# Two experts with fixed places, their token lists made tile by tile, in a mixture-of-experts decoder step

## The reference

```python
def _post_norm_block(x, mix, ...):
    h = _layernorm(DN_ALPHA * x + mix, ln1_g, ln1_b)
    return _layernorm(DN_ALPHA * h + _moe(h, ...), ln2_g, ln2_b)
# _moe: group = argmax of 4 group logits; the 2 best of its 8 experts;
#   weight = p_group * softmax over the two; for each of the 32 experts, its tokens:
#   (silu(x @ w_gate[e]) * (x @ w_up[e])) @ w_down[e] * weight, summed into y[token]
```

## Time and profile before

| | |
|---|---|
| median of 3 runs | 1728.58 us (1725.63 to 1732.63) |
| profiled execution, span | 1724.0 us |
| TensorE / VectorE / ScalarE busy | 1657.2 / 657.7 / 348.0 us |
| HBM read, written | 307.90 MB, 35.51 MB |
| DMA queue of SyncE (q1) | 276.22 MB |
| DMA queue of POOL (q0) | 55.78 MB |

### The profile page before, as it was taken

The page is one execution under the profiler, slowest core; times in us unless marked ns, Lnnn a source line. Parts: engine busy times, 40 slices in busy tenths (PEclk is TensorE's granted clock), DMA queues, the critical chain, the costliest instruction groups (busy, mean ns, idle before and its releaser), DMA issues.

```text
span 1724.0 us, 22514 instructions
## 1 busy us (share of the span) xinstructions
PE 1657.2 (96%) x9293; PEld 1015.9 (59%) x9294; DVE 657.7 (38%) x1382; ACT 348.0 (20%) x679; POOL 163.5 (9%) x169
## 2 busy tenths in 40 slices
PE   8999999999999999999999999999999999999990
PEld 5556777777777666666688555554444444444440
DVE  1446454545542323232577654621121212121225
ACT  1113232223231222212212011111111111111115
POOL 1000000000003321121000000011111111111110
PEclk9999999999999999999899999999999999999995
DMA  7200121211017554342362522578999999999975
GB/s 228 61 21 20 50 62 50 59 53 50 23 64 209 190 170 142 123 158 88 128 218 75 210 104 79 202 302 327 374 394 375 393 397 386 386 390 391 390 289 202
DMA packets 104410, 337.67 MB, mean 196 GB/s; under 512 B 24378, under 2 KB 68482, under 8 KB 87924
## 3 DMA queue, kind: packets, MB, share of 16 engines
q1 hardware_dynamic: 89572, 276.22, 42.4%
q0 software_dynamic: 13568, 55.78, 10.7%
q10 hardware_dynamic: 1168, 4.23, 0.6%
HBM read 307.90 MB, written 35.51 MB: 199 GB/s over the span
## 4 chain that ended last, share of the span: by engine, by line
PE 91%; DMA 5%; DVE 2%; issue 1%; ACT 1%; SPq 0%; POOL 0%; DVEq 0%; POOLq 0%; ACTq 0%
PE psum L1058 12%; PE psum L1172 10%; PE psum L1478 8%; PE psum L1483 7%; PE psum L1360 6%; PE psum L1375 5%; PE psum L1510 4%; PE psum L1504 4%; PE psum L1099 4%; PE psum L962 3%; PE psum L1211 3%; PE psum L1072 2%; DMA arena<-in_w_up 2%; PE psum L1117 2%; PE psum L1491 2%; PE psum L1106 2%
## 5 line engine op out<-in xcount | busy, mean ns | idle before, releaser
L1058 PE MATMUL psum<-arena 128*128 128x258 f32 x896 | 215.3, 384 | 0.0
L1172 PE MATMUL psum<-arena 128*128 128x344 f32 x576 | 182.3, 458 | 0.0
L1058 PEld LDWEIGHTS psum<-arena 128*128 128x128 f32 x896 | 162.8, 190 | 27.9 <-issue 7.0
L1483 PE MATMUL psum<-arena 128*64 128x512 f32 x320 | 141.6, 595 | 0.7 <-ACT arena L1809 0.7
L1484 PE MATMUL psum<-arena 128*64 128x512 f32 x320 | 141.6, 595 | 0.0
L1478 PE MATMUL psum<-arena 128*128 128x512 f32 x320 | 139.8, 595 | 0.2 <-DVE arena L2559 0.2
L1172 PEld LDWEIGHTS psum<-arena 128*128 128x128 f32 x576 | 103.2, 190 | 53.0 <-issue 11.2
L1478 PEld LDWEIGHTS psum<-arena 128*128 128x128 f32 x320 | 60.0, 190 | 72.6 <-issue 72.1
L1360 PE MATMUL psum<-arena 128*128 128x258 f32 x448 | 99.7, 387 | 0.9 <-ACT arena L1766 0.9
L1375 PE MATMUL psum<-arena 128*128 128x512 f32 x224 | 99.2, 595 | 0.0
L1360 PEld LDWEIGHTS psum<-arena 128*128 128x128 f32 x448 | 86.5, 193 | 14.2 <-issue 1.3
(11 more groups left out here) (391 smaller groups left out, 2147.8 us busy)
## 6 DMA issues: line engine op xcount, KB each, us to landing
arena<-in_w_gate SPq DMA_DIRECT2D x32, 2048.0 KB, 20.6
arena<-in_w_up SPq DMA_DIRECT2D x32, 2048.0 KB, 26.3
arena<-in_w_down SPq DMA_DIRECT2D x32, 2048.0 KB, 32.6
arena<-in_w_in SPq DMA_DIRECT2D x33, 512.0 KB, 4.9
gates<-arena SPq DMA_DIRECT2D x16, 516.0 KB, 6.0
arena<-gates SPq DMA_DIRECT2D x16, 516.0 KB, 6.4
arena<-in_x_prompt SPq DMA_DIRECT2D x16, 512.0 KB, 4.6
arena<-in_w_o SPq DMA_DIRECT2D x1, 4096.0 KB, 17.0
```

The costliest lines, as they stand in the source:

```text
L1058: ins = mm(psum[:, BANK[name[0]], 0:QT], held, moved, start=(k == 0 and name in ("X1", "V6", "Y5")), stop=(k == 3), skip_group_check=True)
L1172: ins = mm(psum[:, FB + t, 0:SP3], wring[:, u, k, :], xT[:, k, t * SP3:(t + 1) * SP3], start=(k == 0), stop=(k == KD - 1))
L1483: g = mm(psum[0:64, 2, :], xgT[:, xpar, k, 0:64], wg[:, k, :], start=(k == 0), stop=(k == KD - 1))
```

## The change

1. The two fixed experts come first, then `h h f m ...`; `SOON`, the number of experts with a list of their own, falls from 3 to 2. Their three early matrices and the next three go to other ring places.
2. Their lists are made tile by tile. As their numbers are known, no rank is needed: `first_positions(n)` on TensorE gives each token of tile n its place in the two lists, `first_rows(n)` on VectorE makes a one-hot of it, `first_table(n)` adds the tile to the lists. L1468 and its one-hots are gone.
3. The slot tables of all experts run behind gate and up of the first expert and the turn of the second's rows; VectorE's arithmetic for them lies around the first expert's operations (`swiglu` is cut into `swiglu_gate` and `swiglu_up`, and the copies behind the tables are `slot_lists`).
4. The second expert's matrices are loaded as four parts of 32 partitions each (`load_parts`), without a wait for the row DMAs, the third of them after the lists (`tb_done`). The place under `oh_row` is now that of the third expert's down matrix.
5. `sums` gets `h` unscaled; the weights are divided by ALPHA and the last norm's eps by its square, which leaves the norm's result as it was.
6. Fewer `keep_busy`.

```diff
-SOON = 3
+SOON = 2
-        ring_at = [Z0, Z0 + MAT, Z3 - 64 - 2 * MAT] + [Z3 + i * MAT for i in range(6)] + [Z3 - 64 - MAT]
+        ring_at = [Z3 + i * MAT for i in range(6)] + [Z0, Z0 + MAT, Z3 - 64 - 2 * MAT, Z3 - 64 - MAT]
-        RANK = [next(kinds["h"])] + list(range(FIXED)) + [next(kinds[c]) for c in "hfmhfmhfmhmhfmhfmhfmhfmhmfmqq"]
+        RANK = list(range(FIXED)) + [next(kinds[c]) for c in "hhfmhfmhfmhmhfmhfmhfmhfmhmfmqq"]
@@ SyncE @@
+            def load_parts(j, e):
+                for c in range(4):
+                    part = slice(32 * c, 32 * c + 32)
+                    sp.dma_start(ring(j)[part], matrix(j % 3, e)[part]).then_inc(we_ld[j % RING], 16)
             sp.wait_ge(lg_done, NT)
             sp.wait_ge(h_dve, NT)
+            for m in range(2):
+                load_parts(3 + m, 1)
+            sp.wait_ge(tb_done, 1)
+            load_parts(5, 1)
+            sp.wait_ge(h_out, 16 * NT)
             for q in range(2):
                 sp.wait_ge(ah_out[q], 16 * ((NT - q + 1) // 2))
-            for m in range(3):
-                load_matrix(6 + m, 1)
-            sp.wait_ge(h_out, 16 * NT)
             sp.wait_ge(ord_dve, 1)
-            load_matrix(0, e)
-            load_matrix(1, e)
+            load_matrix(6, e)
+            load_matrix(7, e)
             sp.wait_ge(ws_dve, 1)
-            load_matrix(2, e)
+            load_matrix(8, e)
@@ TensorE @@
+            def first_positions(n):
+                pe.wait_ge(sel_dve, n + 1)
+                mm(psum[:, 6 + n % 2, 64:64 + SOON], tri, m12[:, n, 0:SOON], start=True, stop=False)
+                mm(psum[:, 6 + n % 2, 64:64 + SOON], ones, cum[:, n, 0:SOON], start=False, stop=True).then_inc(pos_done, 1)
+            def first_table(n):
+                pe.wait_ge(oh_dve, n + 1)
+                for k in range(SOON):
+                    ins = mm(psum[:, 2 + k, 0:1], oh_fixed[:, n, k, :], tok_f[:, n:n + 1], start=(n == 0), stop=(n == NT - 1))
+                if n == NT - 1:
+                    ins.then_inc(tb_done, 1)
+                if n >= 2:
+                    first_positions(n - 2)
                 router(n - 1)
...
             pe.wait_ge(r_dve, NT - 1)
-            keep_busy(6, 2)
+            for n in range(NT - 2):
+                first_table(n)
+            first_positions(NT - 2)
             turn_h(NT - 1)
...
-            slot_tables()
-            keep_busy(2, 6)
             rows_in(0)
             for n in range(NE):
                 gate_up(n)
                 if n + 1 < NE:
                     rows_in(n + 1)
                 if n:
                     down_proj(n - 1)
+                else:
+                    slot_tables()
@@ ScalarE @@
-                nc.scalar.mul(ah[0:r, n % 2, :], h_sb[0:r, t, :], ALPHA).then_inc(ah_act, 1)
-                act.dma_start(sums[t * P:t * P + r, :], ah[0:r, n % 2, :]).then_inc(ah_out[n % 2], 16)
+                act.wait_ge(h_dve, n + 1)
+                act.dma_start(sums[t * P:t * P + r, :], h_sb[0:r, t, :]).then_inc(ah_out[n % 2], 16)
@@ VectorE @@
+            def first_rows(n):
+                dve.wait_ge(pos_done, n + 1)
+                stt(out=first_pos[:, n, :], in0=psum[:, 6 + n % 2, 64:64 + SOON], scalar=1.0, in1=m12[:, n, 0:SOON], op0=ALU.add, op1=ALU.mult).then_inc(first_dve, 1)
+                dve.wait_ge(first_dve, n + 1)
+                tt(oh_fixed[:, n, :, :], iota_1.rearrange("p (o c) -> p o c", o=1).broadcast_to([P, SOON, P]),
+                   first_pos[:, n, :].rearrange("p (k o) -> p k o", o=1).broadcast_to([P, SOON, P]), ALU.is_equal).then_inc(oh_dve, 1)
                 link(stt(out=skip, in0=skip, scalar=float(P), in1=cap, op0=ALU.mult, op1=ALU.subtract))
+            rows_right(0)
                 link(tt(r_t, r_t, over_t(skip), ALU.mult))
```

More of the change, by code:

```diff
@@ L1460, in _ @@
+            mm(psum[0:1, 6, 0:NE], iota_p[0:NE], at_rank[0:NE], start=True, stop=True).then_inc(pos_done, 1)
             pe.wait_ge(sel_dve, MORE)
[L1461 to L1468, removed]
@@ L1469, in _ @@
-            ins.then_inc(tb_done, 1)
+            pe.wait_ge(blk_dve, 1)
+            mm(psum[:, 2, 0:NE + 1], more_w[0:NE], tri[0:NE, 0:NE + 1], start=True, stop=True).then_inc(pos_done, 1)
+            keep_busy(4, 1)
             def turn_block(par, rows=P):
@@ L2468, in _, with swiglu_gate, rows_right @@
             nc.vector.tensor_copy(more_w[0:NE], more_i[0:NE].bitcast(I32).broadcast_to([NE, P])).then_inc(sel_dve, 1)
-            for j in range(SOON):
-                link(nc.vector.memset(first_at[:, j:j + 1], float(P * RANK[j])))
-            link(nc.vector.tensor_copy(rank, psum[:, 3, 0:NE]))
+            dve.wait_ge(pos_done, ORDER)
+            nc.vector.tensor_copy(order[0:1].bitcast(I32), psum[0:1, 6, 0:NE]).then_inc(ord_dve, 1)
+            link(nc.vector.tensor_copy(rank, psum[:, 5, 0:NE]))
             width(cap, rank)
             link(tt(r_t, pos, over_t(cap), ALU.is_ge))
-            dve.wait_ge(pos_done, 3)
-            nc.vector.tensor_copy(order[0:1].bitcast(I32), psum[0:1, 4, 0:NE]).then_inc(ord_dve, 1)
             link(stt(out=r_d, in0=over_t(rank), scalar=float(P), in1=pos, op0=ALU.mult, op1=ALU.add))
-            dve.wait_ge(pos_done, 4)
-            link(stt(out=skip, in0=psum[:, 5, 0:NE], scalar=float(NE), in1=rank, op0=ALU.add, op1=ALU.subtract))
+            dve.wait_ge(pos_done, EXTRA)
+            total = ob[:, 0, :]
+            link(nc.vector.tensor_copy(total, psum[:, 2, 1:NE + 1]))
+            link(stt(out=skip, in0=psum[:, 2, 0:NE], scalar=float(NE), in1=rank, op0=ALU.add, op1=ALU.subtract))
             link(stt(out=skip, in0=skip, scalar=float(P), in1=cap, op0=ALU.mult, op1=ALU.subtract))
+            def swiglu_gate(n):
+                dve.wait_ge(gs_act, n + 1)
+                if full(n):
+                    tt(act_t, sig, psum[:, 2, :], ALU.mult).then_inc(gm_dve, 1)
+                else:
+                    if rest(n):
+                        ins = tt(act_x[64:P], sig_x[0:64], psum[0:64, 3, 0:CL], ALU.mult)
+                    if not low(n):
+                        ins = tt(act_t[64:P], sig[0:64], psum[0:64, 2, :], ALU.mult)
+                    ins.then_inc(gm_dve, 1)
+            def rows_right(n):
+                dve.wait_ge(te_done, n + 1)
+                r = room(n)
+                nc.vector.tensor_copy(xgT[:, n % 2, 4:8, 0:r], psum[:, 1, :].rearrange("p (k n) -> p k n", n=P)[:, :, 0:r]).then_inc(te_dve, 1)
+            rows_right(0)
             link(tt(r_t, r_t, over_t(skip), ALU.mult))
@@ L2554, in swiglu, with slot_lists @@
                     ins.then_inc(hu_dve, 1)
-            def rows_right(n):
-                dve.wait_ge(te_done, n + 1)
-                r = room(n)
-                nc.vector.tensor_copy(xgT[:, n % 2, 4:8, 0:r], psum[:, 1, :].rearrange("p (k n) -> p k n", n=P)[:, :, 0:r]).then_inc(te_dve, 1)
+            def slot_lists():
+                dve.wait_ge(ws_done, 1)
+                link(ts(blk_pad, psum[:, 7, 0:NBLK], 0.0, float(T + 1), ALU.is_equal, ALU.mult))
+                stt(out=blk_tok.bitcast(I32), in0=psum[:, 7, 0:NBLK], scalar=-1.0, in1=blk_pad, op0=ALU.add, op1=ALU.add).then_inc(blk_dve, 1)
+                nc.vector.tensor_copy(w_slot, psum[:, 7, NBLK:2 * NBLK]).then_inc(ws_dve, 1)
+                dve.wait_ge(ws_dve, 1)
+                for q in range(4):
+                    nc.vector.tensor_copy(w_rest[32 * q:32 * q + 32, 0:LOW], w_slot[64:96, 0:LOW])
+                    nc.vector.tensor_copy(w_rest[32 * q:32 * q + 32, LOW:NE], w_slot[0:32, LOW:NE])
+                nc.vector.tensor_copy(w_low[64:P], w_slot[0:64, 0:NE]).then_inc(ws_dve, 1)
             def down_right(n):
```

123 lines of the change are left out of this document (58 added, 65 removed).

## The result

Measured side by side, the kernel before takes 1730.67 us (median of 5 runs) and the changed one 1738.26 us (5 runs): ratio 1.005, 95% interval 1.0034 to 1.0066. It is slower by 7.6 us, where a gain of 3.5 had been forecast; the interval lies around the 0.5% that I had named as what can be told apart, so the loss is clear of zero, and whether it passes that mark is open. Each execution takes 1.6 to 1.9 us more than its span, so most of the 4.6 us that the prediction put around the span was scatter between executions; as only differences are carried, no sum hangs on it. The profiled execution has a span of 1733.6 us, 9.6 more than before.

What follows compares the result with a forecast made beforehand. The end was taken to be set by when the weight stream becomes unbroken, by TensorE only through that. M8 issued 10.4 us later, yet expert 5's gate at 1192.8 instead of 1196.3: 1728.6 - 3.5 = 1725 us, range 1716 to 1738.

Steps and rivals of the forecast that it cites:

- First gather: Fetch of the first expert's rows: lands 10.3 us after issue, so that expert starts at 1120.2 (bounds 1114.2 and 1122).
- M8: Weight matrix that waits for the slot tables; its issue was forecast at 1144.7 us, 10.4 later than before.
- M8 is late anyway: Second expert's part loads: at half rate they take 16 us more, which lies in the weight stream's gap.
- Rival B: Second expert's loads: parts at half rate slow the first gather by 6.0 us, giving 1731 us; chance 0.26.
- Norm stage: Between out-projection and router: seven pairs of position matmuls add 3.3 us, all on the path (bounds 0 and 3.7).
- Clock: TensorE at the first expert's start: 2.4 us lost after a thin stretch, 0 if the fillers hold the clock.
- rival C: First gate and up: clock stays at 1.2 GHz throughout, costing 13.9 us instead of 2.4, giving 1737 us; chance 0.12.
- Slot tables and M8: From the first expert's turn through gate, up and tables to M8's issue: 22.1 us, plus 2.4 for the clock.
- rival D: Ranking ahead of the slot tables: ends late again, DVE held by the first turn, giving 1729 us; chance 0.03.
- Return: Weight stream from M8: lands in 8.2 us, seven matrices follow at 5.7 each, expert 5's gate at 1192.8; gain 3.5.
- To the end: After expert 5's gate: all weights land 3.5 us sooner; TensorE waits 5.5 us at expert 27; sum 1725 us.

Runs made afterwards that it cites:

- theory P: Changed kernel, second expert's matrices in two parts of 64 partitions, not four of 32; the theory expected full rate and 1727 to 1730 us. Measured 1738.99 us, ratio 1.006.
- the doubled pairs: Changed kernel with every tile's pair of position matmuls in the norm stage issued twice: 1742.76 us, ratio 1.008.

## Why the prediction was wrong

The failed step is *First gather*, "I take 10.3": it was in flight for 16.7 us, and the bounds of the start, 1114.2 and 1122, didn't hold what came (1130.15, 1127.3 without the drift). Behind it lies a term that the forecast put at nothing: the parts were to cost nothing, as M8 "is late anyway". Rival B had the mechanism, and it was given 0.26. From my own steps to expert 5's gate, forecast to land at 1192.8 and landed at 1206.6:

- drift of this execution: 2.9.
- *Norm stage*, 3.3 forecast: 3.3 measured, right. The gather's issue, 1109.9 forecast, came at 1110.5 without the drift: 0.6, about what the last turn takes more (1.94 us, 1.23 before).
- *First gather*: 16.7, not 10.3: **6.4**. Whole matrices give 10.7 and spread parts at most 9.4, so this is the parts' price. Rival B had 6.0 for it.
- *Clock*, 2.4 forecast: turn and 32 passes cost 0.9 and 1.8 more than at the upper clock, 2.7. The clock did stay down into the first product, as rival C had it (0.50 to 1136 us, 0.92 in the next window and then 1.00); C's 13.9 never came, not even after 7.85 us of idle TensorE. With the steps of *Slot tables and M8*: 24.9 from the first turn to M8's issue, 24.5 forecast: 0.4. VectorE's arithmetic fitted, as said; rival D is out.
- *Return*: M8 landed in 10.1 us, not 8.2 (1.9), and the seven behind it took 5.9 each, not 5.7 (1.5). The gathers that go out beside M8 take their share: with M8 held back until they had passed, it landed in 8.2.

That is 13.7 of the 13.8. Without the drift M8 went out 7.5 us behind its forecast, 17.9 behind the kernel before. Of this the breaks that the stream no longer makes behind M8 give 10.5 back (13.9 in the forecast), and 7.4 are left at expert 5's gate, 6.7 in the span. *To the end* held: 6.07 us a matrix, and the wait of expert 27 is where it was put. Of the 13.3 us between the forecast time of 1725 and the measured 1738.3, 2.1 are that the kernel before took 1730.7 beside it, not 1728.6.

What I had against B was that no row shows a load of 32 partitions. That was no evidence against it. Its size was part luck: B took 4.3 us for a gather into an idle queue and doubled what sharing adds. The runs have 3.3 idle and 10.7 beside whole matrices, which by the same rule makes 18.1; with slow parts the profiles have 16.7, 17.7 and 18.6. And its 1731 was low, as it used my *Return*. The Trainium skill (SBUF — State Buffer, "Door 1: The DMA port swizzle") says that partitions 0 to 31 reach 8 of the 16 ports and 0 to 63 no more, and gives about 218 GB/s for either. The runs agree for both widths: 202 and 225 GB/s in the windows shown for the 64, 197 to 219 for the 32 before the parts run out. By its table of ports every fourth partition lies on all 16, and the spread parts do move at the full rate. For the 64 I hadn't used the page when I set theory P, though it says so in as many words.

My sentence that "M8 is late anyway, so that lies in the gap" was right for the parts' own 16 us: with whole matrices the stream stands still for some 13 us ahead of M8, with the parts for some 3. It was the small transfer beside them that paid, one that everything waits for.

The change would have been even: with whole matrices it is 1727.88 to 1728.93 us. The forecast of a gain of 3.5 was too high even there. In that profile M8 is issued at 1145.1 without the drift, as forecast (1144.7), but lands in 10.2 us and the seven behind it take 6.02 each: the *Return* step alone is 4.2 us short.

## What to carry to other kernels

Read GB/s beside the DMA share: a share of 1.00 at half the bytes was here a transfer with a bad shape. A large load that has time to spare can still be the one to fix, if a small one that has none shares the queues with it: here letting the first rows go ahead of the weights was worth 3.3 us from the gather's issue to M8, and 3.8 in the medians. And where one stream sets the end, a head start given to it counts only if nothing stops it later; look for the next place where it stands still and put there a transfer whose place is already free. Before two medians of a few executions are compared, look at the granted clock of each: here how many had the lower one made more than a third of a difference of 5.5 us.

## What the runs showed of the hardware

- Loads of 2.1 MB in parts of 32 or 64 neighbouring partitions: 197 to 225 GB/s in most windows of 4 us (180 the least, 242 to 258 in three, of the doubled pairs and of the kernel before with parts); in parts of 32 spread over 128 partitions: 412 to 442 once the gather is through; whole: 410 to 446. The DMA share is 0.85 to 1.17 in all of them.
- A gather of 128 rows (512 KB): 3.2 to 3.3 us into idle DMA engines, 9.4 to 10.7 beside full-rate loads, 16.7 to 18.6 beside half-rate ones.
- The profiles of one and the same code differed by up to 7.4 us in a stage at 541 us, and in four of them the last router's 16 passes took 3.47 us, at TensorE's lower level (1.2 GHz, granted clock 0.50), where the others had 1.87 to 2.21. I didn't find what decides either.
